# State scan regrouped: both directions in one product, the solve by factors of the inverse's transpose, the spectrum moved inside the scan

## The chip, the core and the metric

The kernel runs on one core of a Trainium2 chip. Time is device time of one execution in microseconds (us). TensorE (PE) multiplies; its results land in PSUM, from where VectorE (DVE) or ScalarE (ACT) copy them to SBUF; GpSimd (POOL) works on SBUF alone; SyncE (SP) issues transfers. Each engine takes its instructions in written order, and semaphores join the engines.

## The reference, cut to what matters

Two transformer blocks follow each other. The change lies in the first one's token mixer: 256 context tokens and 256 tokens of the sequence, 512 channels in 8 heads of 64, in two directions. Context and sequence share one running state per head and direction; only the sequence is read out.

```python
def rwkv_scan(prep, state0, readout):
    def step(s, inp):
        r_t, k_t, v_t, kk_t, a_t, w_t = inp
        sa = jnp.einsum("dbhij,dbhj->dbhi", s, kk_t)
        s = (s * w_t[..., None, :] - sa[..., :, None] * (kk_t * a_t)[..., None, :]
             + v_t[..., :, None] * k_t[..., None, :])
        y = jnp.einsum("dbhij,dbhj->dbhi", s, r_t) if readout else None
        return s, y
# kd = k * (1 + (a - 1) * k_a), per direction; the output's bonus term uses kd of both
state_c, y_c = rwkv_scan(prep_c, state0, ctx_out)      # context
_, y_l = rwkv_scan(prep_l, state_c, True)              # sequence
# beside it: y = fft2(uf, axes=(1, 3), norm="ortho").real ; rms_norm(y, g)
```

## The kernel before

The order of work is written out by hand for every engine; nothing is planned by a scheduler. The stages are: modulation, the first projection (20 output tiles of 128 channels, `dense_product`, matmuls at L586), the scan, the output product, the feed-forward part, then the second block. The change touches the stretch from about 118 us to 418 us.

The scan goes over 8 chunks of 64 tokens (`STEPS`), 4 of context and 4 of the sequence, in both directions `d`. A token-by-token recurrence inside a chunk is a triangular system of 64 by 64; its inverse is built from products: `grams` makes the system (A and its transpose), `squares_of_near`, `fourths_of_near`, `inverse_of_near` invert the 8 by 8 blocks on the diagonal, `far_part`, `squares_of_far`, `fourths_of_far`, `inverse_of_far` do the rest. This is the "prep" of chunk i. It doesn't need the state. What does is the "chain" of chunk i-1: `held`, `halfway`, `removed`, `state`, and from chunk 4 on `read_out`. PE alternates between both in step i of the loop (i = 1 to 8); in the last step there is only a chain.

Every product is a call of `heads` (L707): 4 pairs of heads, and of each pair one 64x64 matmul on partitions 0 to 63 and one on 64 to 127, so 8 matmuls of 64 moving columns for one direction. An fp32 matmul is two records in the trace, so a product for both directions is 32 records. After each product ACT (`keep`, L1228) or DVE (L1595, L1613, L1618) takes a 128x256 result per direction out of PSUM. POOL stages the decayed keys (`stage_keys`, L2011 to L2024) and adds identities (L2039). Between the products lie pieces of other work for PE: twice a step 8 matmuls on column tiles of 32 (`late_piece`, L685) and two small ones on the full array (`turn_piece`, L694).

The prep of chunk 0 lies between the last output tiles of the projection (`beside_projection`, from tile 13). Then come the Fourier part's `channel_spectrum` (L660) and `token_spectrum` (L671), all ahead of step 1, and its norm (L564) in step 1. After the last step ACT copies the last read-out (`y_kept`, L1338), which releases on DVE the sum of both directions (L1709), the head norm and the gate, up to the output product (L586 again).

## Time and profile before

| | |
|---|---|
| time, median of 3 runs (lowest, highest) | 1392.86 us (1391.18, 1396.64) |
| time of the profiled execution | 1391.15 us |
| its span, first to last instruction | 1389.3 us |
| PE busy | 1290.6 us, 93% |
| DVE, ACT, POOL busy | 543.2, 340.2, 136.7 us |
| scan, first `late_piece` to last read-out | 183.6 to 401.2 us |

PE's busy time counts overlapping matmuls once. "Idle before" is the time an engine stood still ahead of an instruction, with what released it. Times in a timeline row are the start, then the length of the merged group.

### The profile page before, as it was taken

The page shows a single profiled execution, that of the slowest core. Times are in us where ns is not written, and L with a number is a line of the kernel's source. Part 1 is how long each engine was busy: PE and PEld are TensorE (multiplying, and loading weights), DVE is VectorE, ACT ScalarE, POOL GpSimd, SP SyncE. Part 2 cuts the span into 40 slices and gives each one's busy share as a digit, 9 for nine tenths or more (in the row PEclk, how much of TensorE's full clock was granted, in tenths as well). Part 3 has the DMA queues.
Part 4 walks back from the last instruction along what each step waited for, and adds up shares of the span by engine and source line. Part 5 has one row for each costly group of instructions (what it writes and reads, how often), then busy time and mean ns, then how long its engine had stood idle before and what let it go on. Part 6 is the DMA issues. An engine that isn't in the chain of part 4 may idle for free.

```text
span 1389.3 us, 25927 instructions
## 1 busy us (share of the span) xinstructions
PE 1290.6 (93%) x11356; PEld 948.8 (68%) x11356; DVE 543.2 (39%) x1188; ACT 340.2 (24%) x868; POOL 136.7 (10%) x207
## 2 busy tenths in 40 slices
PE   6999999999969999999989999888899949999996
PEld 2446888999958788888878886555477745445433
DVE  1255233443452899980032714454243150001003
ACT  2334233323220321110111113334421112111111
POOL 0002334554100000220000000000000010000000
PEclk9999999999999999999999999999889959999998
DMA  9600021211253343434333232221011385999992
GB/s 392 277 0 31 2 63 64 95 64 65 88 210 139 120 176 128 176 114 160 129 141 129 114 131 112 92 92 61 1 63 61 129 355 241 400 427 429 427 426 99
DMA packets 18544, 223.08 MB, mean 161 GB/s; under 512 B 2112, under 2 KB 3264, under 8 KB 3968
## 3 DMA queue, kind: packets, MB, share of 16 engines
q1 hardware_dynamic: 18032, 220.05, 40.6%
q8 instruction: 90, 1.47, 0.4%
q0 software_dynamic: 256, 1.06, 0.2%
q10 hardware_dynamic: 144, 0.31, 0.1%
q14 instruction: 22, 0.18, 0.0%
HBM read 220.37 MB, written 1.05 MB: 159 GB/s over the span
## 4 chain that ended last, share of the span: by engine, by line
PE 90%; DVE 4%; ACT 3%; DMA 1%; issue 1%; SPq 0%; ACTq 0%; DVEq 0%
PE ps L586 37%; PE ps L707 13%; PE ps L1121 8%; PE ps L934 5%; PE ps L990 4%; PE ps L1165 4%; PE ps L1036 2%; PE ps L1132 2%; PE ps L1102 2%; ACT mem L1430 1%; PE ps L564 1%; PE ps L685 1%; PE ps L781 1%; PE ps L1021 1%; PE ps L1007 1%
## 5 line engine op out<-in xcount | busy, mean ns | idle before, releaser
L586 PE MATMUL ps<-mem 128*128 128x256 f32 (+2 forms) x2096 | 522.4, 407 | 19.6 <-DVE mem L1731 8.3
L586 PEld LDWEIGHTS ps<-mem 128*128 128x128 f32 x2096 | 399.8, 192 | 131.6 <-issue 50.5
L707 PE MATMUL ps<-mem 64*64 64x64 f32 (+1 forms) x5664 | 182.9, 222 | 3.7 <-issue 3.7
L707 PEld LDWEIGHTS ps<-mem 64*64 64x64 f32 x5664 | 176.1, 135 | 14.3 <-issue 13.9
L1760 DVE SCALAR_TENSOR_TENSOR mem<-ps,mem 128x189 f32<-128x189 f32 (+2 forms) x352 | 148.2, 431 | 14.8 <-ACT mem L1376 3.9
L1121 PE MATMUL ps<-mem 128*64 128x512 f32 x512 | 111.6, 592 | 0.6 <-ACT mem L1497 0.5
L1121 PEld LDWEIGHTS ps<-mem 128*64 128x64 f32 x512 | 37.3, 137 | 73.1 <-issue 72.4
L1985 DVE TENSOR_TENSOR mem<-ps,mem 128x512 f32<-128x512 f32 x8 | 5.5, 693 | 187.5 <-PE ps L1121 187.5
L934 PE MATMUL ps<-mem 128*128 128x256 f32 x352 | 77.0, 378 | 0.0
L990 PE MATMUL ps<-mem 128*128 128x272 f32 x256 | 63.1, 398 | 10.8 <-ACT mem L1458 10.8
L934 PEld LDWEIGHTS ps<-mem 128*128 128x128 f32 x352 | 66.5, 189 | 9.7
L1228 ACT ACTIVATE mem<-ps 128x256 f32<-128x256 f32 x128 | 49.2, 384 | 82.6 <-PE ps L707 80.0
L990 PEld LDWEIGHTS ps<-mem 128*128 128x128 f32 x256 | 47.1, 189 | 27.0 <-ACT mem L1458 15.0
L1165 PE MATMUL ps<-mem 128*64 128x512 f32 x256 | 56.7, 595 | 1.4 <-ACT mem L1511 1.4
L1797 DVE RECIPROCAL mem<-mem 128x272 f32<-128x272 f32 x18 | 33.4, 1854 | 57.0 <-ACT mem L1402 57.0
L1618 DVE TENSOR_TENSOR mem<-ps,mem 128x256 f32<-128x256 f32 x64 | 27.1, 424 | 56.4 <-PE ps L707 56.2
L1414 ACT ACTIVATE mem<-ps 128x272 f32<-128x272 f32 x36 | 14.3, 398 | 128.3 <-PE ps L586 117.0
L1376 ACT ACTIVATE mem<-ps,mem 128x256 f32<-128x256 f32 x44 | 24.9, 565 | 83.2 <-POOL mem L2071 61.6
L1165 PEld LDWEIGHTS ps<-mem 128*64 128x64 f32 x256 | 17.7, 136 | 34.6 <-issue 32.0
L1430 ACT ACTIVATE mem<-mem 128x272 f32<-128x272 f32 (+1 forms) x48 | 24.6, 514 | 66.6 <-PE ps L1021 54.9
L1595 DVE TENSOR_TENSOR mem<-ps,mem 128x256 f32<-128x256 f32 (+1 forms) x64 | 26.3, 451 | 35.9 <-PE ps L707 35.5
L1194 ACT ACTIVATE mem<-mem 128x256 f32<-128x256 f32 (+2 forms) x32 | 14.0, 469 | 107.3 <-DVE mem L1896 57.0
(252 smaller groups left out, 1232.8 us busy)
## 6 DMA issues: line engine op xcount, KB each, us to landing
mem<-experts SPq DMA_DIRECT2D x48, 2048.0 KB, 17.5
mem<-weights SPq DMA_DIRECT2D x44, 2048.0 KB, 8.0
mem<-late_ada SPq DMA_DIRECT2D x16, 1024.0 KB, 5.3
mem<-weights SPq DMA_DIRECT2D x3, 1536.0 KB, 6.8
mem<-tokens SPq DMA_DIRECT2D x1, 2048.0 KB, 12.6
mem<-consts SPq DMA_DIRECT2D x1, 1504.0 KB, 23.5
out<-mem SPq DMA_DIRECT2D x1, 1024.0 KB, 4.8
mem<-consts POOLq DMA_DIRECT2D x1, 776.0 KB, 5.6
```

The source lines that it names most:

```text
L586: last = mm(bank(j % banks)[:, 0:nn], w[:, kc, c * P:(c + 1) * P], rr(kc), start=kc == 0, stop=kc == KD - 1)
L707: last = mm(out[hp, j], lhs[hp, j], rhs[hp, j], start=i == 0, stop=i == len(terms) - 1)
L934: last = mm(bank(4 * (1 - half) + c)[:, 0:TX], block_view(b)[:, kc, c * P:(c + 1) * P], g[:, 8 * q + kc, :], start=q == 0 and kc == 0, sto ...
L990: last = mm(bank(7)[:, 0:L], w[:, kc, c * P:(c + 1) * P], u[:, kc, :], start=kc == 0, stop=kc == KD - 1)
L1036: last = mm(bank(attended_bank(hd))[:, 0:L], V[0:nt, t, e, :], WT[hd % 2][0:nt, t, :], start=t == 0, stop=t == 2)
L1102: last = mm(o, utok[:, t, c * P:(c + 1) * P], sel_flat[:, t, q * quad:(q + 1) * quad], start=t == 0, stop=t == 2)
L1121: last = mm(bank(b)[64 * e:64 * e + 64, :], xs[:, kc, 2 * (i % 2) + e, :], w[e][:, kc, :], start=kc == 0, stop=kc == KD - 1)
L1165: last = mm(bank(3 + half)[64 * e:64 * e + 64, :], hidT[:, f, 64 * e:64 * e + 64], w[e][:, f, half * 512:(half + 1) * 512], start=f == 0, ...
L1228: A(dst[d], by_pair(b(s, d), width), ACT.Copy, scale=scale).then_inc(turns_of(name + "_kept"), 1)
L1430: last = A(ee[n % 3][0:nq, m, :], src, ACT.Exp, scale=scale, bias=stat[n % 3][0:nq, 2 + m:3 + m], accum_out=stat[n % 3][0:nq, 4 + m:5 + m])
L1760: n(stt(out=o, in0=src[:, r0 + dy:r1 + dy, c0 + dx:c1 + dx], scalar=prm("ffn_conv", tap * 2 * NG + j), in1=o, op0=ALU.mult, op1=ALU.add))
L1797: V_.reciprocal(rs2, rt2).then_inc(S("head_recips"), 1)
```

## The change

Six things are done together.

1. `heads` makes a product of both directions in one call: 16 matmuls, direction 0 into PSUM bank b and direction 1 into bank b+1. With `crossed`, direction 1 takes its operands from one half of the partitions and puts its result on the other half, so that the four matmuls of a head pair use four different quadrants of the array. In the prep of chunks 0 to 3, and in all of their chains, nothing is crossed; `turned` and `third_factor` are never crossed.
2. The inverse is no longer multiplied out. `W8` and the raised M, M2, M4 (each plus the identity, transposed) are applied one after the other in the chain: `first_factor`, `second_factor`, `third_factor`, then `spread_solution` per direction (stationary 64 rows by 128 columns), `state` and `read_out` (stationary 128 rows by 64 columns). In the sequence's chunks the three factors have 128 moving columns.
3. ACT and DVE take out both directions with one instruction of 128x512 (128x1024 for a wide factor; 64 partitions in `keep_spread`, `keep_state`).
4. `token_spectrum` is cut into two calls per step of steps 1 to 4, its norm moves to step 5, `late_piece` and `turn_piece` move, `turn_piece(i, 1)` into the next step.
5. The per-token key factors are made once for all chunks ahead of chunk 0: 8 ACT instructions, 4 on DVE, 12 on POOL, of 128x512 each. `stage_keys` has 3 instructions per direction in place of 7.
6. SP copies the values next to the state's rows (4 transfers a chunk, `place_values`), and the bonus term starts from the finished keys, behind the last read-out on DVE.

```diff
-            def heads(out, *terms):
+            def heads(b, width, lhs, rhs, crossed=True):
+                out = over_banks(b, width)
                 for j in range(NJ):
-                    for i, (lhs, rhs) in enumerate(terms):
-                        for hp in (slice(0, 64), slice(64, 128)):
-                            last = mm(out[hp, j], lhs[hp, j], rhs[hp, j], start=i == 0, stop=i == len(terms) - 1)
+                    for hp in (LOW, HIGH):
+                        mm(out[hp, 0, j], lhs[hp, 0, j], rhs[hp, 0, j], start=True, stop=True)
+                    for hp, to in ((LOW, HIGH), (HIGH, LOW)) if crossed else ((LOW, LOW), (HIGH, HIGH)):
+                        last = mm(out[to, 1, j], lhs[hp, 1, j], rhs[hp, 1, j], start=True, stop=True)
                 return last
+            def product(s, name, b, lhs, rhs, width=C, crossed=True):
+                heads(b, width, lhs, rhs, crossed and s >= READ_FROM).then_inc(turns_of(name), 1)
...
+            def spread_solution(s, d):
+                if d == 0:
+                    waits(s, "X3_kept", "reads_kept", "gram_kept")
+                else:
+                    waits(s, "for_state0", "for_values0")
+                width = C if s < READ_FROM else 2 * C
+                for j in range(NJ):
+                    o = [bank(CHAIN + hp)[:, j * width:(j + 1) * width] for hp in range(2)]
+                    for hp, rows in ((0, LOW), (1, HIGH)):
+                        mm(o[hp], KX[s % 2][rows, d, j, C:3 * C], RX[s % 2][rows, d, j, C:C + width],
+                           start=True, stop=False)
+                    for hp, rows in ((0, LOW), (1, HIGH)):
+                        last = mm(o[hp], GR[rows, j, 2 * d:2 * d + 2, :].rearrange("p a c -> p (a c)"),
+                                  XB[rows, d, j, 0:width], start=False, stop=True)
+                last.then_inc(turns_of("spread%d" % d), 1)
...
-            fourths_of_far(0)
+            turned(0)
+            squares_of_far(0)
             channel_spectrum(2)
             channel_spectrum(3)
-            inverse_of_far(0)
-            token_spectrum(0)
-            token_spectrum(1)
+            fourths_of_far(0)
             for i in range(1, STEPS + 1):
+                if i < STEPS:
+                    removals(i)
+                if i >= 2:
+                    turn_piece(i - 2, 1)
+                first_factor(i - 1)
                 late_piece(i - 1, 0)
                 if i < STEPS:
-                    grams(i)
-                held(i - 1)
-                if i < STEPS:
                     squares_of_near(i)
...
+                second_factor(i - 1)
+                turn_piece(i - 1, 0)
                 if i < STEPS:
                     fourths_of_near(i)
...
+                if i <= NJ:
+                    token_spectrum(i - 1, 0)
+                elif i == NJ + 1:
+                    waits(i - 2, "state0", "state1")
+                    norm_sums("four", squares_f, NJ, TX, SIDE)
+                third_factor(i - 1)
+                if i < STEPS:
+                    part_of_near(i)
+                spread_solution(i - 1, 0)
                 if i < STEPS:
                     inverse_of_near(i)
...
+                if i <= NJ:
+                    token_spectrum(i - 1, 1)
                 if i < STEPS:
                     far_part(i)
...
+                spread_solution(i - 1, 1)
+                if i < STEPS:
+                    turned(i)
+                    state(i - 1)
+                    squares_of_far(i)
+                if i - 1 >= READ_FROM:
+                    read_out(i - 1)
+                late_piece(i - 1, 1)
+                if i < STEPS:
                     fourths_of_far(i)
```

On POOL, at the head of the program, this stood ahead of the prep of chunk 0 (the staging of direction 0, then of direction 1 in the same way):

```order
6 L2011 ISA
7 L2011 TENSOR_TENSOR mem<-mem 128x4x64
8 L2012 TENSOR_TENSOR mem<-mem 128x4x64
9 L2014 TENSOR_TENSOR mem<-mem 128x4x64
10 L2016 TENSOR_TENSOR mem<-mem 128x4x64
11 L2019 TENSOR_TENSOR mem<-mem 128x4x64
```

Now this stands there (L2211, L2215 and L2216 make the factors for all chunks, L2227 puts identities, L2236 to L2238 stage one direction of chunk 0):

```order
7 L2211 TENSOR_TENSOR mem<-mem 128x512 x4
8 L2215 TENSOR_TENSOR mem<-mem 128x512
9 L2216 TENSOR_TENSOR mem<-mem 128x512
10 L2215 TENSOR_TENSOR mem<-mem 128x512
11 L2216 TENSOR_TENSOR mem<-mem 128x512
12 L2215 TENSOR_TENSOR mem<-mem 128x512
13 L2216 TENSOR_TENSOR mem<-mem 128x512
14 L2215 TENSOR_TENSOR mem<-mem 128x512
15 L2216 TENSOR_TENSOR mem<-mem 128x512
16 L2227 COPY mem<-mem 128x4x64 x2
17 L2236 TENSOR_TENSOR mem<-mem 128x4x64
18 L2237 TENSOR_TENSOR mem<-mem 128x4x64
```

Twelve instructions of 128x512 and two copies have moved ahead of the first chunk's keys.

On ACT, one step over chunks of the sequence looked like this before (L1228 takes out a product of one direction, L1338 the read-out, L1233 a `late_piece`, L1220 and L1221 the decays):

```order
121 L1221 ACTIVATE mem<-mem 128x256
122 L1220 ACTIVATE mem<-mem 128x4x64
123 L1221 ACTIVATE mem<-mem 128x256
124 L1228 ACTIVATE mem<-ps 128x256 x10
125 L1338 ACTIVATE mem<-ps 128x4x64 x2
126 L1228 ACTIVATE mem<-ps 128x256 x2
127 L1233 ACTIVATE mem<-ps 128x256
128 L1228 ACTIVATE mem<-ps 128x256 x4
129 L1241 ACTIVATE mem<-ps 128x512 x2
```

In the changed kernel the middle of such a step is (L1325 takes out both directions: X3, Q1, the turned keys, the first spread, W8 and M, then the decays and the second spread; L1320 and L1321 are the decays):

```order
189 L1325 ACTIVATE mem<-ps 128x1024
190 L1325 ACTIVATE mem<-ps 128x512
191 L1325 ACTIVATE mem<-ps 128x8x64
192 L1325 ACTIVATE mem<-ps 64x1024
193 L1325 ACTIVATE mem<-ps 128x512 x2
194 L1320 ACTIVATE mem<-mem 128x4x64
195 L1321 ACTIVATE mem<-mem 128x256
196 L1325 ACTIVATE mem<-ps 64x1024
197 L1325 ACTIVATE mem<-ps 128x2x4x128
```

W8 (the first of the two in row 193) now stands behind the 64x1024 of the first spread.

On DVE, behind the scan's last instructions (L1618, the last sum of the prep), the bonus term (L1698 to L1706) and the sum of both directions (L1709) stood so:

```order
163 L1613 COPY mem<-ps 128x256 x4
164 L1618 TENSOR_TENSOR mem<-ps,mem 128x256 x4
165 L1698 TENSOR_TENSOR mem<-mem 128x1024
166 L1701 TENSOR_SCALAR mem<-mem 128x256 x4
167 L1703 TENSOR_TENSOR mem<-mem 128x1024
168 L1706 SCALAR_TENSOR_TENSOR mem<-mem 128x256 x4
169 L1709 TENSOR_TENSOR mem<-mem 128x1024
```

and stand now (L1822 and L1824 take out the second spread, L1837 the last read-out, L1912 and L1915 are the bonus term, L1918 the sum of both directions):

```order
180 L1822 COPY mem<-ps 64x8x64
181 L1824 TENSOR_TENSOR mem<-ps,mem 64x8x64
182 L1837 COPY mem<-ps 128x4x64 x2
183 L1912 TENSOR_TENSOR mem<-mem 128x1024
184 L1915 SCALAR_TENSOR_TENSOR mem<-mem 128x256 x4
185 L1918 TENSOR_TENSOR mem<-mem 128x1024
```

The bonus term is shorter by two groups, and the last read-out is now copied by DVE ahead of it.

## Rows read from the trace of the kernel before

**Rows 1.** The page's chain that ended last, shares of the span.

```profile
PE 90%; DVE 4%; ACT 3%; DMA 1%; issue 1%; SPq 0%; ACTq 0%; DVEq 0%
```

**Rows 2.** Busy time by stretch; columns: PE, PEld, DVE, ACT, POOL, granted clock, DMA.

```profile
330.00:360.00 30.00, 29.14 (x862) 27.58 (x860) 12.05 (x30) 8.73 (x23) 13.98 (x22) 1.00 0.21 69
```

**Rows 3.** PE's timeline, first `late_piece` of steps 1 to 5 and 8.

```profile
183.60 1.07 PE L685 MATMUL ps<-mem 128*32 128x256 f32 x16
...
213.82 1.07 PE L685 MATMUL ps<-mem 128*32 128x256 f32 x16 [0.86 <-ACT mem L1349]
...
241.53 1.07 PE L685 MATMUL ps<-mem 128*32 128x256 f32 x16 [0.86 <-ACT mem L1349]
...
267.58 1.07 PE L685 MATMUL ps<-mem 128*32 128x256 f32 x16 [0.86 <-ACT mem L1349]
...
295.26 1.07 PE L685 MATMUL ps<-mem 128*32 128x256 f32 x16 [0.86 <-ACT mem L1349]
...
386.70 1.07 PE L685 MATMUL ps<-mem 128*32 128x256 f32 x16 [0.86 <-ACT mem L1349]
```

**Rows 4.** PE's groups by form; busy us, mean ns of one record.

```profile
L586 PE MATMUL ps<-mem 128*128 128x256 f32 x976 | 218.0, 383 | 11.8 <-DVE mem L1731 8.3 <-ACT mem L1363 3.4
L707 PE MATMUL ps<-mem 64*64 64x64 f32 x5408 | 170.9, 219 | 3.7 <-issue 3.7
L1121 PE MATMUL ps<-mem 128*64 128x512 f32 x512 | 111.6, 592 | 0.6 <-ACT mem L1497 0.5
L685 PE MATMUL ps<-mem 128*32 128x256 f32 x256 | 18.0, 399 | 8.4 <-ACT mem L1349 6.0 <-DMA mem<-late_ada 2.4
L707 PE MATMUL ps<-mem 64*64 64x128 f32 x256 | 16.7, 269 | 0.0
L630 PE MATMUL ps<-mem 64*128 64x512 f32 x32 | 9.0, 641 | 0.0
L913 PE MATMUL ps<-mem 128*128 128x16 f32 x16 | 1.9, 258 | 0.0
```

**Rows 5.** Timeline around one `late_piece` of the sequence's part.

```profile
316.45 1.07 PE L685 MATMUL ps<-mem 128*32 128x256 f32 x16
...
317.45 3.81 PEld L707 LDWEIGHTS ps<-mem 64*64 64x64 f32 x128 [0.41 <-issue]
```

**Rows 6.** PE's timeline beside and behind the projection.

```profile
137.35 2.08 PE L707 MATMUL ps<-mem 64*64 64x64 f32 x64
139.36 3.72 PE L586 MATMUL ps<-mem 128*128 128x256 f32 x16
...
176.48 7.20 PE L671 MATMUL ps<-mem 128*128 128x256 f32 x32
```

**Rows 7.** Groups by form of ACT, DVE and POOL that price the copies.

```profile
L1241 ACT ACTIVATE mem<-ps 128x512 f32<-128x512 f32 x16 | 9.6, 597 | 22.5 <-PE ps L781 22.5
...
L1595 DVE TENSOR_TENSOR mem<-ps,mem 128x512 f32<-128x512 f32 x8 | 5.5, 691 | 3.1 <-PE ps L707 3.1
L1703 DVE TENSOR_TENSOR mem<-mem 128x1024 f32<-128x1024 f32 x1 | 1.2, 1227 | 0.0
...
L2031 POOL TENSOR_TENSOR mem<-mem 128x512 f32<-128x512 f32 x16 | 16.6, 1043 | 51.6 <-PE ps L781 40.6 <-PE ps L586 11.0
L2020 POOL TENSOR_TENSOR mem<-mem 128x256 f32<-128x256 f32 x16 | 11.8, 738 | 0.0
```

**Rows 8.** Timeline, ACT's last of the small projections (L1249).

```profile
116.89 1.27 ACT L1249 ACTIVATE mem<-ps,mem 128x512 f32<-128x512 f32 x2
```

**Rows 9.** Timeline of the last step and what follows the scan.

```profile
393.90 1.93 PE L685 MATMUL ps<-mem 128*32 128x256 f32 x16 [2.42 <-DMA mem<-late_ada]
...
401.21 1.23 DVE L1709 TENSOR_TENSOR mem<-mem 128x1024 f32<-128x1024 f32 x1 [10.30 <-ACT mem L1338]
...
406.16 1.42 DVE L1719 SCALAR_TENSOR_TENSOR mem<-ps,mem 128x256 f32<-128x256 f32 x4 [3.38 <-PE ps L887]
...
417.93 7.12 PEld L586 LDWEIGHTS ps<-mem 128*128 128x128 f32 x26 [8.75 <-DVE mem L1731]
```

More of the change, by code:

```diff
@@ L245, in two_blocks @@
         ka_rest = whole.take(NJ)
-        ka_rest2 = whole.take(NJ)
+        whole.take(NJ)
         gain12 = whole.take(KD)
@@ L295, in two_blocks @@
         ms = Places(mem, ring_at, ring_at + RING * WBLK)
[L296 to L302 removed]
+        pair = (2, NJ, C)
+        pairs = (2, NJ, 2 * C)
+        triples = (2, NJ, 3 * C)
+        FIRST, SECOND, THIRD = slice(0, C), slice(C, 2 * C), slice(2 * C, 3 * C)
```

826 lines of the change are left out of this document (468 added, 358 removed).

## The prediction

> **What bounds the kernel now.** I read the page's chain first: 90% of what ended last is PE [rows 1]. Then the busy time by stretch: in the sequence's half of the scan PE is busy for 29.14 of 30 us at full clock, DVE for 12.05, POOL for 13.98 [rows 2]. So the scan costs what PE's instructions cost. Then PE's timeline, to mark the steps [rows 3]: 183.60 us for step 1, then steps of 30.2, 27.7, 26.1 and 27.7 us, and steps 5, 6 and 7 with (386.70 - 295.26) / 3 = 30.5 us each. Last, the groups by form [rows 4], for how much of the array works at once.
>
> A record of 128 by 128 with 256 columns takes 218.0 / 976 = 0.223 us. On column tiles of 32 it takes 18.0 / 256 = 0.070: more than three run at once. On column tiles of 64, 512 columns take 111.6 / 512 = 0.218, about what 256 take on the full array: two at once. L707 uses two quadrants on the diagonal: 170.9 / 5408 = 0.032, in a dense stretch 2.01 / 64, and with its ramp taken off 0.029 [rows 4, 6].
>
> **Prices.** A product of both directions is 32 records.
> - On the diagonal: 0.93 us narrow (64 columns). Wide (128 columns) the record is 16.7 / 256 = 0.065 with its ramp, 0.056 without [rows 4], so 1.8 us.
> - On four quadrants no row exists. Bounds: 0.93 (no gain over the diagonal) and 0.47 (half). Column tiles overlap fully with the same rows (L685), and row tiles overlap (L707), each with its own weights, so I take 0.47, and 0.9 wide.
> - A spread: 32 records, stationary 64 by 128. 128 columns of weights set the pace where few columns move: L913 has 1.9 / 16 = 0.119 us per record. L630 shows two row tiles at work together: 9.0 / 32 = 0.28 a record where one alone would need about twice the 0.22 of 256 columns [rows 4]. 16 pairs of 0.11 are 1.8 us, wide or narrow.
> - A change of the array's tiling: a `late_piece` takes 1.00 us from 316.45 to 317.45 for 4 x 0.22 us of work, and the weights' row shows 0.41 us idle [rows 5]. With the way in counted like the way out, I take 0.3 too much, 1.15 in all. Every visit in another form gets 0.3: spread 2.15, `state` or `read_out` 1.2, half a token piece 1.25, `turn_piece` 0.68.
> - A copy: ACT 0.60 us for 128x512 and about 1.0 for 1024, DVE 0.69 and 1.23 [rows 7]. From a product's last matmul to the next that needs it I count 0.3 more.
>
> The Trainium skill speaks against the 0.47. "TensorE: Matmul & The Clock Gate", Part 3, says that a weight load overlaps with running matmuls only if its row group differs; two of the four quadrants share their rows. By that rule the price would be 0.93 and the result rival B's. The trace disagrees where it can: all column tiles of L685 span all 128 rows and more than three run at once [rows 4].
>
> **Ahead of step 1: -5.5 us.** The 7.20 us of `token_spectrum` go [rows 6]. Until ACT's last L1249 ends at 118.2 [rows 8] nothing can start; then 8 factors on ACT, and behind the first of them 12 instructions of 128x512 on POOL. POOL has 1.04 us for one with a broadcast operand, 0.74 for 256 columns with two full ones [rows 7]; I take 1.2 (bounds 1.04 and 1.5): 14.4 us. With two identities and 6 staging instructions of 0.7 the keys are there at about 139, PE wants them at 137.35 [rows 6]: 1.7 us of new wait, at most 5. The six prep stages between projection tiles were 2.01 us each; now they are 2.9, 2.0, 1.1, 1.1, 1.1, 2.9: 1 us less, with the 3.65 us of the tiles as cover for the copies. `turned(0)` 1.8, the two squares 1.9 with 1 us of wait for the grams, two pairs of L660, `M4T` 0.9: step 1 begins at 178.1 instead of 183.6.
>
> **Steps 1 to 3: +5.6 us.** Prep: 10 narrow and 3 wide products, 9.3 + 5.4 = 14.7. Chain: three factors 2.8, two spreads 4.3, `state` 1.2. Other: two late pieces 2.3, two turns 1.4, two token halves 2.5. Sum 29.2: PE's load fell from 368 to 352 matmuls, but the weights of the spreads, five more visits and the spectrum eat it. Step 1 has one turn less, but `reads_staged` of chunk 1 stands on DVE behind `M4T` of chunk 0 and two memsets, 2.4 us: 31.0. Together 89.6 against 84.0 [rows 3].
>
> **Steps 4 to 7: -13.2 us.** Prep is now 12 x 0.47 + 2 x 0.9 + 1.8 (`turned`) = 9.2. Step 4 with a context chunk's chain: 23.7 and 1 us of waits, 24.7. Steps 5 to 7: factors 0.9 + 0.9 + 1.8, spreads 4.3, `state` and `read_out` 2.4, late and turn 3.7, prep 9.2: 23.2 of load. Here PE no longer covers the copies. I walked one step: 1.0 us before `removals`, since DVE copies read-out and stages reads (4 x 0.42) ahead of `M4T`; 0.4 before the third factor (X2 is 1024 wide on DVE); 1.3 before `M`, since ACT copies the 64x1024 of the first spread, then W8. That gives 26.0. Step 5 has the Fourier sums, 27.2; step 6 starts behind the Fourier norm on DVE (3.4 us, of which 2 show), 28.0. Sum 24.7 + 27.2 + 28.0 + 26.0 = 105.9 against 386.70 - 267.58 = 119.1.
>
> POOL is not late: about 11 us of the 26, though it stands until the second spread of the chunk before releases the keys' buffer, and `MT_raised` behind it is due 7 us into the next step. ACT has 13, DVE 15. The 32 small transfers of `place_values` stand on SP between pieces that are 10 us apart; their waits are met before the next piece is due.
>
> **The last step and behind it: +6.0 us.** No prep covers the chain. First turn and `M4T` copy 1.0, X1 0.9, late piece 1.2, 0.2 until X1 is out, X2 0.9, 1.5 until X2 is out, X3 1.8, 1.4, spread 1.9, 1.7 (DVE has two instructions of 0.69), spread 1.8, 1.7, read-out 1.1, its copy 1.1: about 18.2 us. Before it was 401.2 - 386.7 = 14.5 [rows 3, 9], including 2.42 us of wait for a transfer that now has the whole step to land. +3.7. Behind it: bonus term 1.23 + 1.67 now stands ahead of the sum of both directions on DVE, which was free at once; it took 5.0 us from that sum to L1719 [rows 9], since PE was late with the bonus sums; now about 6.3: +1.3. The clock: before, PE fell to the half clock after 2.42 us of waiting, and L685 took 1.93 in place of 1.07 [rows 9]. Gaps of 1.4 to 1.7 us, five of them, invite that again: +1.0 (bounds 0 and 4).
>
> Sum: -5.5 + 5.6 - 13.2 + 6.0 = -7.1. The profiled execution took 1391.15 us, so 1384.1; it lies 1.7 under the median of the runs, on whose scale that is 1386. Everything from 417.93 on is as before.
>
> **Rivals.**
> - A, the forecast: 1386, own range 1380 to 1392.
> - B, slower: four quadrants don't run at once. Each step 4 to 7 has 12 x 0.47 + 1.8 = 7.4 us more in prep, and steps 5 to 8 1.8 in the factors; waits of about 1 to 2.7 us a step vanish under it. 6.4 + 6.5 + 4.5 + 6.5 + 1.8 is 26: 1412. It decides from about 0.7 us per crossed product on: 16 products' worth in each of 4 steps, 0.25 us more each, less some 10 us of waits, eat the 7.1. For it: nowhere in the trace do records follow closer than 0.029 us over a whole product. Against it: L685. The Trainium skill, same page, Part 2, gives a least distance of about 25 ns between matmuls; by that a crossed product would be 0.80 us and the time an estimated 1400.
> - C, between: quadrants overlap but the waits grow, since each copy now covers both directions and its consumer waits for all of it. 1 us more in each of 8 steps and 2 more for POOL's keys: 1396. For it: the copies' queue on ACT behind a 64x1024. Against it: all engines but PE are at most 60% busy.
> - D, better: the waits I walked and the 0.3 a visit partly hide, since weights for the next form load early, and the clock holds: 0.15 for 60 visits is 9: 1376.
>
> **How the numbers follow.** A 0.48, B 0.12, C 0.20, D 0.20. Half a percent is 7 us, about what a measurement here can tell: faster means under 1385.9, where D and nearly half of A lie, 0.43. Slower means over 1399.8: B and the far part of C, 0.20. The rest, 0.37, is within. The range 1374 to 1400 leaves out B and the tail of D.
>
> **What would show it.** Crossed products in steps 4 to 7: 32 records in about 0.6 us with ramp (A), 1.0 (B). Steps 2 and 3 29 us apart from late piece to late piece, steps 6 and 7 28 and 26. The first scan product at 139, step 1 at about 178, the last read-out kept near 393, and the output product's first weights near 411. The forecast is wrong if the steps of the context gain, or if a step of the sequence has more than 4 us of idle PE.

## The result, and the profile after

The changed kernel takes 1402.29 us (median of 4, 1401.07 to 1403.96), the kernel before 1392.82 (1391.18 to 1396.64). The ratio is 1.0058, with a 95% interval of 1.0042 to 1.0074: half a percent slower. The forecast was 1386 in a range of 1374 to 1400, so it had the wrong sign and the range missed too. The profiled execution took 1403.96 us, 1.7 above its median, and its span is 1401.8. The profiled one before took 1391.15, 1.7 below its median, with 1389.3. So the two traces are 12.5 us apart where the medians are 9.5 apart: 3 us of what is laid out below belong to the two executions and not to the change.

The page's chain and PE's total, which answer to [rows 1]. PE has 4.6 us less to do than before and still ends later; DVE, ACT, DMA and POOL have taken shares of the chain.

```profile
PE 1286.0 (92%) x10396; PEld 931.8 (66%) x10396; DVE 548.7 (39%) x1113; ACT 359.7 (26%) x845; POOL 123.7 (9%) x139
...
PE 85%; DVE 5%; ACT 4%; DMA 3%; POOL 1%; issue 1%; SPq 0%; ACTq 0%; DVEq 0%
```

PE's timeline with the first `late_piece` (L749) of steps 2 to 8, which answers to [rows 3]. In this kernel the piece stands 4 to 5 us into its step, behind two products and the first factor. What is new is the bracket: before, these pieces waited 0.86 us for ACT, and only the second piece of the last step waited for its transfer [rows 9]. Now all seven wait for the transfer, 7.3 us in all.

```profile
218.90 1.07 PE L749 MATMUL ps<-mem 128*32 128x256 f32 x16 [0.43 <-DMA mem<-late_ada]
248.24 1.07 PE L749 MATMUL ps<-mem 128*32 128x256 f32 x16 [0.45 <-DMA mem<-late_ada]
277.79 1.08 PE L749 MATMUL ps<-mem 128*32 128x256 f32 x8 [1.57 <-DMA mem<-late_ada]
305.30 1.07 PE L749 MATMUL ps<-mem 128*32 128x256 f32 x16 [0.31 <-DMA mem<-late_ada]
335.16 1.07 PE L749 MATMUL ps<-mem 128*32 128x256 f32 x16 [1.16 <-DMA mem<-late_ada]
363.69 0.64 PE L749 MATMUL ps<-mem 128*32 128x256 f32 x8 [1.02 <-DMA mem<-late_ada]
391.51 1.94 PE L749 MATMUL ps<-mem 128*32 128x256 f32 x16 [2.34 <-DMA mem<-late_ada]
```

Busy time by stretch, one of the context's steps and one of the sequence's; columns as in [rows 2], to which the second answers. The context keeps PE busy (29.57 of 30 us), the sequence doesn't (24.58 of 29): 4.4 us idle, above the 4 us that the prediction named as a sign of being wrong.

```profile
210.00:240.00 30.00, 29.57 (x682) 26.60 (x680) 9.90 (x18) 11.32 (x24) 10.73 (x13) 1.00 0.26 82
...
324.00:353.00 29.00, 24.58 (x754) 21.42 (x752) 17.14 (x27) 13.07 (x23) 10.23 (x13) 1.00 0.26 85
```

A product on four quadrants in step 6, `removals` of chunk 6. Each row is two records. Four records start within 20 ns, the next four 0.11 us later and every further four 0.06 us later. In a dense run 32 take 0.46 to 0.47 us; here, with the way in and out, it is 0.63 until the next form begins at 332.36.

```profile
331.73 0.27 PE L771 MATMUL ps<-mem 64*64 64x64 f32 x2 [1.27 <-DVE mem L1791]
331.74 0.27 PE L773 MATMUL ps<-mem 64*64 64x64 f32 x2
331.84 0.22 PE L771 MATMUL ps<-mem 64*64 64x64 f32 x2
331.85 0.23 PE L773 MATMUL ps<-mem 64*64 64x64 f32 x2
331.90 0.23 PE L771 MATMUL ps<-mem 64*64 64x64 f32 x2
...
332.20 0.23 PE L773 MATMUL ps<-mem 64*64 64x64 f32 x2
332.36 0.61 PE L758 MATMUL ps<-mem 128*128 128x2 f32 x4
```

Ahead of step 1: DVE's four products of the keys, two of POOL's factors (alone, and beside DVE) and the first scan product, which stood at 137.35 before [rows 6]. Behind them the wait of step 1.

```profile
125.80 6.18 DVE L1843 TENSOR_TENSOR mem<-mem 128x512 f32<-128x512 f32 x4
123.90 1.26 POOL L2215 TENSOR_TENSOR mem<-mem 128x512 f32<-128x512 f32 x1
126.36 1.72 POOL L2215 TENSOR_TENSOR mem<-mem 128x512 f32<-128x512 f32 x1
140.83 0.54 PE L771 MATMUL ps<-mem 64*64 64x128 f32 x4 [3.68 <-POOL mem L2238]
...
184.22 0.44 PE L771 MATMUL ps<-mem 64*64 64x128 f32 x4 [2.90 <-DVE mem L1777]
```

The last step begins at 387.13, its read-out at 408.64, and the output product's first weights are at 428.55, in place of 417.93 [rows 9]. The stretch from 389 to 404 us has a granted clock of 0.66; the same 15 us of the kernel before had 0.89.

```profile
387.13 0.61 PE L758 MATMUL ps<-mem 128*128 128x2 f32 x4
408.64 1.15 PE L909 MATMUL ps<-mem 128*64 128x64 f32 x32 [1.54 <-ACT mem L1325]
428.55 0.50 PEld L650 LDWEIGHTS ps<-mem 128*128 128x128 f32 x2 [8.75 <-DVE mem L1940]
```

That stretch, by the view of busy time:

```profile
389.00:404.00 15.00, 10.69 (x124) 8.26 (x116) 1.61 (x2) 2.82 (x4) 0.00 (x0) 0.66 0.31 119
```

Between these marks, in us of the span, with step 4 beginning at 272.87. Step 1 is counted from 181.3, where PE has done the work ahead of it and begins to wait for 2.90 us:

| part | before | after | forecast | measured |
|---|---|---|---|---|
| to the beginning of step 1 | 183.6 | 181.3 | -5.5 | -2.3 |
| steps 1 to 3 | 84.0 | 91.6 | +5.6 | +7.6 |
| steps 4 to 7 | 119.1 | 114.3 | -13.2 | -4.9 |
| last step, to the output's first weights | 31.2 | 41.4 | +6.0 | +10.2 |
| behind it | 971.4 | 973.2 | 0 | +1.8 |

The parts sum to 12.4, the spans differ by 12.5. The forecast's sum was -7.1, so on the scale of the traces 19.5 us are to be explained: 3.2, 2.0, 8.3, 4.2 and 1.8.

### The profile page after: what moved, and what is told of

Read it like the earlier page. It is cut to its first block, busy times and chain, and to the rows that moved or that the text cites. A ratio compares the mean times of both kernels' runs of the same rounds, so it can differ in the third digit from the quotient of the medians.

```text
span 1401.8 us, 23797 instructions
## 1 busy us (share of the span) xinstructions
PE 1286.0 (92%) x10396; PEld 931.8 (66%) x10396; DVE 548.7 (39%) x1113; ACT 359.7 (26%) x845; POOL 123.7 (9%) x139
## 4 chain that ended last, share of the span: by engine, by line
PE 85%; DVE 5%; ACT 4%; DMA 3%; POOL 1%; issue 1%; SPq 0%; ACTq 0%; DVEq 0%
PE ps L650 36%; PE ps L1220 8%; PE ps L1033 5%; PE ps L771 5%; PE ps L1089 4%; PE ps L1264 4%; PE ps L773 3%; PE ps L1135 2%; DMA mem<-late_ada 2%; PE ps L1231 2%; PE ps L1201 2%; ACT mem L1601 1%; PE ps L628 1%; PE ps L875 1%; PE ps L749 1%; PE ps L878 1%
## 5 line engine op out<-in xcount | busy, mean ns | idle before, releaser
L771 PE MATMUL ps<-mem 64*64 64x64 f32 (+1 forms) x2176 | 134.3, 241 | 17.7 <-ACT mem L1325 4.1
L773 PE MATMUL ps<-mem 64*64 64x64 f32 (+1 forms) x2176 | 132.1, 240 | 0.3 <-issue 0.3
L771 PEld LDWEIGHTS ps<-mem 64*64 64x64 f32 x2176 | 104.6, 138 | 34.0 <-issue 15.7
L1220 PE MATMUL ps<-mem 128*64 128x512 f32 x512 | 111.4, 592 | 0.5 <-ACT mem L1668 0.5
L773 PEld LDWEIGHTS ps<-mem 64*64 64x64 f32 x2176 | 104.7, 138 | 1.3 <-issue 1.3
L1325 ACT ACTIVATE mem<-ps 128x512 f32<-128x512 f32 (+4 forms) x111 | 71.8, 658 | 108.8 <-PE ps L773 83.7
L1220 PEld LDWEIGHTS ps<-mem 128*64 128x64 f32 x512 | 37.0, 137 | 73.0 <-issue 72.3
L2243 POOL TENSOR_TENSOR mem<-mem 128x512 f32<-128x512 f32 x32 | 38.7, 1211 | 93.2 <-DVE mem L1787 44.7
## 6 DMA issues: line engine op xcount, KB each, us to landing
mem<-tokens SPq DMA_DIRECT2D x1, 2048.0 KB, 12.4
```

The source lines that it names most:

```text
L771: mm(out[hp, 0, j], lhs[hp, 0, j], rhs[hp, 0, j], start=True, stop=True)
L773: last = mm(out[to, 1, j], lhs[hp, 1, j], rhs[hp, 1, j], start=True, stop=True)
L1220: last = mm(bank(b)[64 * e:64 * e + 64, :], xs[:, kc, 2 * (i % 2) + e, :], w[e][:, kc, :], start=kc == 0, stop=kc == KD - 1)
L1325: A(dst, src, ACT.Copy, scale=scale).then_inc(turns_of(name), 1)
L2243: tt(dst, src, eye, ALU.add).then_inc(turns_of(name), 1)
```

## The experiments

All ran beside the kernel before, at 1393 to 1394 us in each set. "State to state" is the time between the first records of `state` in neighbouring steps; in the changed kernel it is 29.3 and 29.5 in steps 2 and 3 and 28.5 to 28.7 from step 4 on. Each trace is one execution, and which stretches run at half clock differs between executions (see the clock, below), so single steps are compared with care.

### Is a product on four quadrants worth its price?

**all_diagonal**

```
-                heads(b, width, lhs, rhs, crossed and s >= READ_FROM).then_inc(...)
+                heads(b, width, lhs, rhs, False).then_inc(...)
```

> The changed kernel with every product of the scan on the diagonal quadrants, those of chunks 4 to 7 too. Theory (four quadrants do run at once, 0.62 us a narrow product in place of 1.0, 0.92 a wide one in place of 1.84): in steps 4 to 7 12 x 0.4 + 2 x 0.92 = 6.6 us more each, two wide factors in each of steps 5 to 8 1.84 more, together 34 us of PE; about 4 us of waits a step vanish under it, so 1418 to 1428, and the steps of the sequence some 33 us. Rival (the quadrants take turns after all, the loss is there): within 5 us of the changed kernel's 1402.

Measured: 1420.89 us, ratio to the kernel before 1.0191 (1.0164 to 1.0219). From state to state 32.5, 34.4, 33.3 and 33.6 us. So the four quadrants save 18.6 us, and the regrouping without them costs 27. Rival B is out as a cause. In its sequence PE is busy for 32.02 of 33 us: with longer products nearly all waits vanish.

```profile
335.00:368.00 33.00, 32.02 (x744) 29.34 (x742) 16.02 (x27) 12.38 (x23) 9.42 (x11) 1.00 0.22 74
```

**all_crossed**

```
-                heads(b, width, lhs, rhs, crossed and s >= READ_FROM).then_inc(...)
+                heads(b, width, lhs, rhs, crossed).then_inc(...)
```

> The changed kernel with the products of chunks 0 to 3 on four quadrants too, only turned and X3 on the diagonal. Theory (a product costs PE 0.4 us less narrow, 0.92 less wide, and copies set in only where nothing covers them): 10 x 0.4 + 2 x 0.92 = 5.8 us of prep less and 0.8 of factors less in each of steps 1 to 3, 3 us less beside the projection, of which about 2 us a step come back as waits for copies: 1383 to 1392. Rival (the chain of product, copy, product sets the step, so that PE's time only turns into idle time): 1399 to 1403, with 4 us or more of idle PE in each of steps 2 and 3.

Measured: 1386.78 us, ratio 0.9954 (0.9939 to 0.9970): 15.5 us under the changed kernel. State to state falls to 26.4 and 26.1 in the context, by 3.2 of the 6.6 us of PE work that the expectation takes out; the sequence takes 30.0 us in step 4, 10 us of them at half clock, and 28.1 to 28.9 from there, as before. The trace is of an execution 2.6 us above the median. The waits for `late_ada` grow from 7.3 to 10.6 us.

```profile
PE ps L749 <- DMA mem<-late_ada: 10.6, 7, 2.4
```

### What sets the sequence's steps?

**pieces_apart**

```
                 if i < STEPS:
                     far_part(i)
+                late_piece(i - 1, 1)
                 spread_solution(i - 1, 1)
...
                     read_out(i - 1)
-                late_piece(i - 1, 1)
```

> The changed kernel with late_piece(i-1, 1) between far_part and the second spread, in place of behind the state and the read-out, so that its successor's transfer has some 10 us in place of 5. Theory (the 7.3 us of PE before L749 are the transfer, and two half-clock stretches hang on them): those waits go to 0, 2 to 4 us come back as waits for copies that they covered: 1392 to 1398. Rival (PE waits there anyway, for the copy of X1 and the masks on DVE): 1400 to 1403, with the idle time moved to the products behind.

Measured: 1402.06 us, ratio 1.0058 (1.0039 to 1.0078): nothing gained. The transfer is no longer waited for. In its place PE waits 6.2 us for L1787, DVE's copy of `M2T`, which the piece behind the read-out had covered (0.9 us before). Step 4 takes 2.1 us less, but the changed kernel's step 4 holds 3.4 us at half clock and this one none. Step 6 gains nothing (28.6), and steps 5 and 7, each with a half-clock stretch, take 31.3 and 30.7 us. From the last state to the last read-out it is 19.9 us in place of 26.6, without the piece, the wait for its transfer and the half clock.

```profile
PE ps L771 <- DVE mem L1787: 6.2, 6, 2.0
PE ps L771 <- ACT mem L1325: 4.1, 4, 1.1
PE ps L771 <- DVE mem L1791: 3.8, 4, 1.3
```

**dve_order**

```
-                if 1 <= i < STEPS - 1:
-                    stage_reads(i + 1)
                 if i >= 1:
                     keep_state(i - 1)
                 keep(i, "M2T", B4)
+                if 1 <= i < STEPS - 1:
+                    stage_reads(i + 1)
+                keep_raised(i, "M4T", 1, M4TI)
                 if i - 1 >= READ_FROM:
                     keep_read(i - 1)
                 if READ_FROM <= i + 1 < STEPS:
                     stage_own_reads(i + 1)
-                keep_raised(i, "M4T", 1, M4TI)
```

> The changed kernel with DVE's queue reordered at the end of a step: stage_reads behind the copy of M2T, and the copy of the read-out and the own reads behind the copy of M4T, where they stood ahead. Theory (in the steps of the sequence a step is 28.5 us with or without the waits for transfers, since DVE's queue ahead of the copies of M2T and M4T sets when the next step can begin): the 1.27 us ahead of the second product of removals in steps 6 to 8 fall to about 0.4, steps 5 to 7 take 27.7 us from state to state, and the time is 1396 to 1400. Rival (PE's own work and the other waits set it, what goes here comes back in front of keys_turned or X1): 1401 to 1404 with steps of 28.5.

Measured: 1404.67 us, ratio 1.0067 (1.0045 to 1.0089). The mirror image: the wait for L1791 falls from 3.9 to 0.7 us, and that for the transfer grows from 7.3 to 9.1. The next piece stands behind it, and its transfer of 5.6 to 6.1 us starts when the last piece has ended, whatever DVE does. The staged reads (L1777), moved back in the queue, are waited for 4.8 us in place of 2.9.

```profile
PE ps L749 <- DMA mem<-late_ada: 9.1, 5, 2.5
...
PE ps L771 <- DVE mem L1777: 4.8, 5, 2.9
...
PE ps L771 <- DVE mem L1791: 0.7, 2, 0.3
```

**both_apart**: both edits above together.

> The changed kernel with DVE's queue as in dve_order and the late piece behind far_part as in pieces_apart, so that both releasers go but the piece doesn't stand at W8. Theory (two waits overlapped, each removed alone showed the other; together they are worth 4 to 5 us, and the place at W8 up to 1.1 us a step more): 1396 to 1399, steps of 27 to 27.7 us. Rival (the gain was the place at W8 alone): 1401 to 1404, steps of 28.5. Rival (the place has no part in it): 1393 to 1395.

Measured: 1397.64 us, ratio 1.0026 (1.0011 to 1.0041). 4.6 us less, where each edit alone gave none. Steps 4 to 7 take 26.4, 27.5, 28.6 and 27.0 us, steps 2 and 3 1.1 more than in the changed kernel. The clock has a part in this: this trace has no half clock in steps 4 to 7, those of the single edits have 13.7 us each.

**pieces_at_w8**: DVE's queue as in dve_order, and the piece where PE waits for the copy of `W8`.

```
                 if i < STEPS:
                     inverse_of_near(i)
+                late_piece(i - 1, 1)
```

> As the run before, and late_piece(i-1, 1) between the products W8 and M in place of behind the read-out: there PE waits 1.12 us for ACT's copy of W8, and its successor's transfer has 15 us. Theory (a piece is worth its place only where PE would wait anyway; behind the read-out the copies are early now): steps 5 to 7 take 26 to 27 us, the waits for late_ada are gone, the last step is 3 to 6 us shorter: 1388 to 1395. Rival (the piece uncovers the copy of M2T as in the run that moved it alone, or the clock falls instead): 1398 to 1403.

Measured: 1394.55 us, ratio 1.0003 (0.9988 to 1.0017): 7.7 us less than the changed kernel, 3.1 of them from the place. `state` of steps 5, 6 and 7 in PE's timeline, the last two 25.7 us apart (353.55 and 382.09 in the changed kernel, 28.5 apart). The step between the first two holds a half-clock stretch and a wait of 2.7 us for DVE's masks (L1765). The DVE rows behind them show what that wait is: the Fourier norm (L1702, L1705) stands ahead of the masks from 332.64 to 336.09. It is the 2 us that the prediction gave to step 6. In the changed kernel the wait for the transfer covers it, so step 6 gains nothing from an edit that removes the transfer's wait alone.

```profile
326.07 1.15 PE L897 MATMUL ps<-mem 128*64 128x64 f32 x31
355.04 1.15 PE L897 MATMUL ps<-mem 128*64 128x64 f32 x32
380.77 1.15 PE L897 MATMUL ps<-mem 128*64 128x64 f32 x31
...
332.64 1.74 DVE L1702 RECIPROCAL mem<-mem 128x256 f32<-128x256 f32 x1
334.42 1.67 DVE L1705 SCALAR_TENSOR_TENSOR mem<-mem 128x256 f32<-128x256 f32 x4
...
337.44 0.27 PE L771 MATMUL ps<-mem 64*64 64x64 f32 x2 [2.73 <-DVE mem L1765]
```

**pieces_seq**: as pieces_at_w8, but `if i > 3` for the new place and `if i <= 3` for the old.

> As pieces_at_w8, but in steps 1 to 3 the piece stays behind the state. Theory (there PE has no wait between W8 and M, and the piece covered 0.9 us of the copy of M2T): steps 2 and 3 take 29.4 us in place of 30.5, and 1388 to 1392. Rival (other waits of those steps show instead, or the clock): 1393 to 1396.

Measured: 1394.99 us, ratio 1.0005 (0.9994 to 1.0017). Steps 2 and 3 are at 29.5 and 29.4 again, as the theory had it. But steps 4 and 5 take 30.3 and 29.6 in place of 26.4 and 26.5, each with a half-clock stretch (278 to 282 and 302 to 309 us), and step 4 waits 1.5 us for a transfer, since the last piece of step 3 stands at the old place. The gain in steps 2 and 3 shows in the trace, not in the total.

**late0**: the other piece of a step moved, behind the third factor, and its turn ahead of the second spread.

```
                 first_factor(i - 1)
-                late_piece(i - 1, 0)
...
                 third_factor(i - 1)
+                late_piece(i - 1, 0)
```

> The changed kernel with late_piece(i-1, 0) behind the third factor in place of the first, its turn ahead of the second spread: the transfer has 13 us in place of 5, and the other late piece stays where it covered the copy of M2T. Theory (after the run with the other piece moved: the wait was also the cover of DVE's masks): the 7.3 us of L749 go to 0, L771 waits 4 to 5 us more for L1765 and the copy of X1, the last step gains the 2.3 us: 1396 to 1400. Rival (nothing else is late there): 1392 to 1395. Rival (a wait for a wait again): 1401 to 1403.

Measured: 1407.98 us, ratio 1.0104 (1.0088 to 1.0120), worse than all three expectations. The transfer's wait is gone. The products wait more for ACT's copies, for the masks (L1765) and for the copy of `X2` (L1816), and 5.6 us stand as "issue". The scan has about as much half clock in this trace as in the changed kernel's (21 us against 20.5), and it is the fastest of the five executions. How the loss splits stays open.

```profile
PE ps L771 <- ACT mem L1325: 6.0, 5, 1.4
...
PE ps L771 <- DVE mem L1765: 2.9, 2, 2.4
PE ps L771 <- DVE mem L1816: 2.6, 3, 1.3
```

### Ahead of step 1

**reads_first**

```
+                if i == 0:
+                    dve.wait_ge(S("proj"), 19)
+                    stage_reads(1)
                 keep_raised(i, "M4T", 1, M4TI)
                 if i == 0:
-                    dve.wait_ge(S("proj"), 19)
...
-                    stage_reads(1)
```

> The changed kernel with stage_reads(1) on DVE ahead of the copy of M4T and the two memsets. Theory: the 2.90 us of PE's wait before removalsT of chunk 1 go to less than 0.5, and the half clock from 185.4 to 188.8 us with them (1.7 us): 1397 to 1400. Rival (keys of POOL or the decays of ACT are late next, the clock falls anyway): 1401 to 1403.

Measured: 1400.17 us, ratio 1.0054 (1.0035 to 1.0072), 2.1 us less, just above the theory's range and within the spread of the runs: not settled. In its trace, of an execution 3.4 us above the median, the wait of 2.90 us is gone, and the stretch from 184 to 190 us is at full clock. Two later stretches are at half clock that were at full clock in the changed kernel (1.00 in both).

```profile
184.00:190.00 6.00, 6.00 (x170) 5.35 (x166) 2.57 (x5) 2.76 (x6) 2.52 (x2) 1.00 0.17 31
301.00:307.00 6.00, 6.00 (x96) 4.26 (x100) 1.29 (x2) 1.39 (x3) 2.52 (x2) 0.50 0.39 130
362.00:368.00 6.00, 5.15 (x120) 3.48 (x116) 0.69 (x3) 2.03 (x4) 2.76 (x3) 0.54 0.42 126
```

**keys_shared**

```
+            for j in range(NJ):
+                key_removals(1, j)
             conv(7)
+            for j in range(NJ):
+                key_removals(0, j)
...
-                n(tt(iclr[:, 0, j, :], iclr[:, 0, j, :], kk[:, j, :], ALU.mult))
```

> The changed kernel with the four products iclr(d=0) x kk on DVE in place of POOL, and those of d=1 on DVE ahead of conv(7). Theory (POOL's 12 and DVE's 4 instructions of 128x512 slow each other, 1.26 to 1.72 us on POOL, and POOL ends last): keys on POOL by about 136, the wait of 3.7 us before the first scan product under 0.5, and that product near 137.3; 1396 to 1399. If only the place of the clock's fall moves: 1399 to 1401. Rival (DVE's reads are late instead, the contention grows): first scan product at 140 or later, 1401 to 1404.

Measured: 1401.88 us, ratio 1.0062 (1.0046 to 1.0077): a wait under another name. The one for POOL is gone, but `conv(7)` now comes late, and PE's turning of the values waits for it (L1739).

```profile
131.74 1.44 PE L715 MATMUL ps<-mem 64*64 64x64 f32 x42 [3.60 <-DVE mem L1739]
```

**keys_dve**: the same four products on DVE, but all eight behind `conv(7)`.

> The changed kernel with the four products iclr(d=0) x kk on DVE behind its own four, not on POOL, and nothing moved ahead of conv(7). Theory (12 instructions on POOL at 1.26 to 1.72 us are what is late ahead of the first scan product, as the prediction's price of 1.2 was too low beside a busy DVE): POOL ends some 4 us earlier, DVE's reads are staged by 137 to 138, the 3.68 us of wait fall under 1; 1396 to 1400. Rival (DVE's reads come at 139 or later, the same wait under another name): 1401 to 1403.

Measured: 1397.16 us, ratio 1.0027 (1.0013 to 1.0041), 5.1 us less. The wait for POOL fell from 3.68 to 1.58 us, less than I had it, since POOL now stands still for 3.69 us and goes on at 135.53, just behind the last of DVE's eight (135.41), for which its code waits. The first scan product begins at 140.82, where it began before: this execution was 2.1 us late ahead of every edit (L694 at 116.59 in place of 114.51), and against that mark the product is 2.1 us earlier. The other 3 us of the gain can't be put down to the edit: the stretch at half clock behind the product did not come, and the last step has 3.4 us at half clock in place of 10.3. DVE's eight take 7.53 us: up to 1.76 each beside POOL, 0.68 each for the five that run while POOL stands. The changed kernel's four took 6.18, 1.55 each, beside a POOL that never paused.

```profile
127.88 7.53 DVE L1843 TENSOR_TENSOR mem<-mem 128x512 f32<-128x512 f32 x8
...
125.99 5.86 POOL L2216 TENSOR_TENSOR mem<-mem 128x512 f32<-128x512 f32 x4
135.53 1.18 POOL L2227 COPY mem<-mem 128x256 f32<-128x256 f32 x2 [3.69 <-issue]
...
140.82 0.44 PE L771 MATMUL ps<-mem 64*64 64x128 f32 x4 [1.58 <-POOL mem L2238]
```

### The clock and the last step

**warm**

```
+                if s == 0:
+                    pe.wait_ge(S("values_kept"), 4)
+                    fill(14, 4)
+                elif s == 1:
+                    fill(10, 2)
```

`fill(n, b)` is n matmuls of `ident` by `ident` into bank b; 5 and 7 more stand ahead of two late pieces, 3, 4 and 5 in the last step.

> The changed kernel with matmuls of 128 by 128 with 128 columns (two records of some 0.11 us each) that nothing reads, put into PE's waits: 14 ahead of the first scan product, 10 ahead of removalsT of chunk 1, 5 and 7 ahead of the transfers of late pieces (3, 0) and (7, 0), 3, 4 and 5 ahead of the two spreads and the read-out of the last step. They add 48 x 0.22 = 10.6 us of PE work. Theory (the 20.7 us that the changed kernel spends at half clock between 140 and 401 us cost it some 9 us, and idle time sets them off): most stretches at half clock go and the time is 1391 to 1397, with more PE work than before. Rival (the clock costs little, or falls elsewhere all the same): 1400 to 1407.

Measured: 1410.32 us, ratio 1.0110 (1.0093 to 1.0127). The theory fell, and the time is above the rival's range too: the filled places ran at full clock, others did not. Steps 3 and 5, which hold no filler, took 33.7 and 34.2 us, with half clock in 249 to 256 and 317 to 320; 5.6 us of idle PE are put down to "issue" and stay unexplained.

**warm_last**: the 19 matmuls of the last step alone.

> The changed kernel with 19 matmuls that nothing reads (4.2 us of PE work) in the waits of the last step alone: 7 ahead of the late piece, 3 and 4 ahead of the spreads, 5 ahead of the read-out. Theory (PE idle for 2.34 us and then at half clock for 10 us is what makes this step 5 us longer than forecast): the step at full clock, 26.6 us from the last state to the last read-out become 22 to 24, total 1398 to 1401. Rival (the clock falls there whatever PE does, and the matmuls come on top): 26.5 us or more, 1402 to 1406.

Measured: 1403.42 us, ratio 1.0063 (1.0040 to 1.0086). The last step behaves as the theory has it: full clock from 384 to 410, and 23.0 us from the last state to the last read-out in place of 26.6, though 4.2 us of work were added. The total shows none of it. Two stretches of steps 5 and 7 are at half clock that were at full clock in the changed kernel, and these steps take 30.6 and 30.0 us. The same two stretches are at half clock in reads_first, an edit elsewhere. The rows are of warm_last; from 304 to 310 us it runs 88 records where the changed kernel ran 180.

```profile
384.00:410.00 26.00, 23.51 (x470) 20.14 (x469) 8.78 (x14) 8.94 (x13) 1.33 (x2) 1.00 0.24 83
304.00:310.00 6.00, 5.84 (x88) 4.12 (x88) 1.39 (x3) 1.20 (x2) 2.52 (x2) 0.51 0.44 149
365.00:371.00 6.00, 5.15 (x117) 3.56 (x120) 0.86 (x2) 2.19 (x4) 2.52 (x2) 0.55 0.44 126
```

**bonus_fill**: DVE's bonus term ahead of `keep_factor(STEPS - 1)`, its sums on PE ahead of the two spreads of the last step.

```
+                if i == STEPS:
+                    bonus_sums(0)
                 spread_solution(i - 1, 0)
```

> The changed kernel with the bonus term of DVE (1.23 + 1.68 us) ahead of the last step's copies and its eight matmul records ahead of the two spreads of the last step. Theory: DVE stood idle for 7.5 us there and PE for 1.12 and 1.48; the sum of both directions starts 2.9 us earlier and everything behind it: 1398 to 1400. Rival (PE's spreads move back by the 1.75 us of records, at half clock 3.5, and eat it): 1401 to 1404.

Measured: 1400.83 us, ratio 1.0063 (1.0040 to 1.0087), 1.5 us less than the changed kernel, within the spread of the runs: not settled. In its trace, of an execution 5.4 us above the median, the output's first weights come 17.4 us behind the last read-out's first record in place of 19.9, 2.5 us sooner where 2.9 were expected. The last step itself is as slow as ever (26.5).

### Together

**best_crossed**: all_crossed, reads_first, dve_order, the piece at `W8` and bonus_fill.

> Everything at once: the products of all chunks on four quadrants, reads of chunk 1 ahead of the copy of M4T, DVE's queue as in the first run of this set, the piece between W8 and M, the bonus term and its sums inside the last step. Theory (all_crossed at 1387 in the runs before, less some 8 us of waits for late_ada and M4T, less 2.9 us of bonus term): 1370 to 1380. Rival (each copy is now longer than the product that should cover it, and the clock falls in the waits): 1383 to 1390.

Measured: 1373.11 us, ratio 0.9858 (0.9829 to 0.9888).

**best2**: keys_dve added.

> best_crossed with the four products on DVE as in keys_dve. Theory: the first scan product at 137 to 138 in place of 140.9, and the half clock behind it gone: 1367 to 1371. Rival (as for keys_dve): 1372 to 1375.

Measured: 1370.09 us, ratio 0.9828 (0.9806 to 0.9851). It beats both kernels, by 23.8 us (the one before, in the same set) and 32.2 us (the changed one, in another). PE has 28.6 us less work than in the changed kernel, DVE and ACT about the same, POOL 6 less. That keys_dve adds 3 us to best_crossed isn't settled: the intervals of the two ratios overlap.

```profile
PE 1257.4 (92%) x10396; PEld 903.4 (66%) x10396; DVE 547.7 (40%) x1117; ACT 359.2 (26%) x845; POOL 117.3 (9%) x135
```

## Why the prediction was wrong

**What held.** Prices on PE were close. Narrow diagonal products of both directions take 0.98 to 1.03 us with their ramp, a wide one 1.8, a spread 1.93 to 1.99, `state` 1.08, a late piece 1.00, a turn 0.54. Steps 2 and 3 add up to 29.2 in the forecast and are 29.3 and 29.5. Column and row tiles together do work at once, as I had inferred from L685 against the Trainium skill's rule that a weight load overlaps with running matmuls only if its row group differs ("TensorE: Matmul & The Clock Gate", Part 3). By that rule all_diagonal would have cost nothing; it cost 18.6 us. The least distance of about 25 ns in Part 2 isn't what this trace shows either: four crossed records start within 20 ns. The waits that I walked in a step of the sequence are there too: 1.0 forecast and 1.27 measured ahead of `removals`, 1.3 and 1.12 ahead of `M`. From the last read-out's copy (410.6) to the output's weights it is 18.0 us, as forecast.

**The step that failed.** It is the last sentence on steps 4 to 7: transfers "stand on SP between pieces that are 10 us apart; their waits are met before the next piece is due". That is true from the first piece of a step to the second, 20 us on. From the second piece of one step to the first of the next it is 5.7 us (357.97 to 363.69). A transfer of `late_ada` takes 4.7 to 6.0 us from issue to landing, 5.1 in the median, and those with four transfers of `place_values` right behind them 5.5 to 5.7. I had looked at the small transfers and not at `late_ada`'s own turnaround. Steps 4 to 7 lose 4.1 us to it directly, the last step 2.3.

**How far that goes.** From 272.87 to 387.13, steps 4 to 7, PE is busy for 100.2 us and idle for 14.1. The forecast of 105.9 was 94.5 of load and 11.4 of waits. The transfers are 4.1 of the idle time, all other waits 10.0, less than I had walked. So of the 8.3 us too little, 2.6 are idle time and 5.7 are load: the wait is the step that failed, but the larger part is a load set too low.

**What the experiments add.** The table has the four steps from the state of step 3 to that of step 7. PE runs the same 2931 records in them (2930 in the last row), so what its busy time has above both_apart's is in the main the clock.

| run | length | PE busy | idle | granted clock |
|---|---|---|---|---|
| changed kernel | 114.30 | 100.25 | 14.05 | 0.99 |
| pieces_apart | 117.01 | 103.66 | 13.35 | 0.94 |
| dve_order | 117.70 | 103.83 | 13.87 | 0.94 |
| both_apart | 109.57 | 98.14 | 11.43 | 1.00 |
| pieces_at_w8 | 107.64 | 99.25 | 8.39 | 0.98 |

The wait for the transfer removed alone takes 0.7 us off the idle time, that for `M4T` alone 0.2, both together 2.6, and with the piece at its best place 5.7. So in the idle time one wait does hide the other. In the totals this is not shown cleanly: the traces of the single edits have 5.5 and 5.7 us more of busy time than the one of both. How much of the 4.6 us of both_apart is the pair, and how much the clock, stays open.

**A size that was off.** Twelve narrow products a step were charged 0.47, the price in a dense run. I had written 0.6 "with ramp" into the list of what to look for and left it out of the sum. Where a product follows another one it takes 0.47 to 0.58, alone 0.62; at a mean of 0.58 (my estimate from step 6) it is 1.3 us a step, 5 us over steps 4 to 7. The wide products on four quadrants take 0.92 to 1.10 where I had 0.9, some 0.5 us a step in steps 5 to 7. Visits and spreads were cheaper than charged and give 1 us a step back. The half clock from 277.6 to 281.0 took nearly 2 more. Together that is some 5 of the 5.7 us of load.

**Steps 1 to 3: +7.6 for +5.6.** Nearly all of it is step 1, 32.7 us (to 214.0) for 31.0. The reads of chunk 1 were waited for 2.90 us, as planned within 0.5, and half clock followed from 185.4 to 188.8, which no term had. (The forecast's own sum is 89.4, from 31.0 and twice 29.2, not 89.6.)

**The last step: +10.2 for +6.0.** Where it keeps its clock and has no wait for the transfer (pieces_apart), it takes 17.8 us from its beginning to the read-out's copy; I had 18.2. The piece stands in one of the waits there, so the walk of the chain was near the mark, not confirmed to the tenth. The wait I had declared gone ("has the whole step to land") is the failed step again, since the piece's predecessor ends at the end of the step before. The clock, +1.0 with bounds of 0 and 4, was too small. dve_order keeps the order of PE's work and 2.5 us of waits in that place, against 2.7, and its last step is at full clock: 17.9 us from its beginning to the read-out, where the changed kernel takes 21.5. So the clock is 3.6 us here.

**Ahead of step 1: -2.3 for -5.5.** POOL's 1.2 us per factor became 1.26 alone and 1.72 beside DVE, and DVE's 0.69 became 1.55. That contention, within my bound of 5 us for the wait, made it 3.68 where I had 1.7. keys_dve shows 2.1 us of it taken back. The half clock from 141 to 144.5 took 1.7 more, and I had no term for it.

**Behind the last mark: +1.8 for 0.** PE runs the same 4188 records there in 909.9 us in place of 908.2, with 75.5 us at half clock in place of 73.7. No instruction there was changed, so this belongs to the executions.

**The clock as a term.** Between 140 and 401 us the changed kernel has 20.5 us at half clock, the kernel before about 3.4. I had priced the clock in one place. In reads_first, warm and warm_last the stretch went from the place that was repaired and another came elsewhere, so a price per place is the wrong form. But these are single executions, and the clock differs between executions of the same instructions. The stretch from 30 to 44 us lies ahead of every edit, PE is busy in it for the same 11.95 us in both traces below, and the granted clock is 0.88 in the changed kernel and 0.51 in all_crossed. The scan of all_crossed begins 4.1 us later for it (144.90 for 140.83). The rows are of the changed kernel and of all_crossed.

```profile
30.00:44.00 14.00, 11.95 (x45) 5.89 (x38) 6.79 (x18) 8.47 (x19) 0.00 (x0) 0.88 1.01 416
30.00:44.00 14.00, 11.95 (x39) 6.33 (x29) 6.79 (x18) 7.80 (x18) 0.00 (x0) 0.51 1.01 418
```

The eight executions of reads_first have mean clocks from 0.961 to 0.968 and take 1397.57 to 1405.79 us, the two slowest at 0.961. So a stretch that is at half clock in one variant's trace and not in another's isn't yet an effect of the edit. What decides where the clock falls is not settled here. all_diagonal, with almost no waits in its sequence, has no half clock from 190 us to the end of the scan, but neither has both_apart from 191 us to its last read-out, with 11.4 us of idle PE in the table above. Idle time may invite the falls; no run shows it alone, and the fillers of warm did not prevent them.

**Chances.** Case C (1396) lay nearest and had 0.20, but its number was near by luck. It was right about POOL's keys, 2 us of new wait. It put the rest on waits for the larger copies, and in steps 4 to 7 the waits other than the transfer's came to less than forecast; the load and the clock it did not have. Beyond 1400 I had allowed mainly B, the one case that these runs exclude.

## What to carry to other kernels

When a change takes work off the bounding engine, list for each transfer on its path the shortest distance between the end of the last use of its buffer and the next use, not the mean one: cover is lost there first. When a wait is removed and the idle time stays, look for what ends just behind it and remove both before judging either, and put a small independent piece of work where the engine would wait anyway. Charge short products with their ramp. Compare the clock of several executions before a stretch at half clock is put down to an edit, and compare idle time and busy time apart.

## What the hardware showed unexpectedly

- Four quadrants with their own weights start four records in 20 ns and 32 in 0.46 to 0.47 us, twice the rate of the diagonal pair (0.93), and a product alone in its form pays 0.16 us on top.
- DVE and POOL slow each other on 128x512 instructions with both operands in memory: POOL 1.26 to 1.72 us, DVE 0.68 (in keys_dve, while POOL stands) to 1.55 on average and 1.76 at most.
- Half-clock stretches lie in other places from trace to trace, also ahead of every edit (granted clock 0.88 to 0.51 from 30 to 44 us for the same instructions). The mean granted clock is 0.956 to 0.966 in the profiled executions of the changed kernel and its variants (0.970 before) and 0.956 to 0.970 in all of theirs. An edit worth 3 us in its own step can therefore be invisible in the total, in either direction.
